# Read orders of the moving operand in the feed-forwards, shifted split weights, and an odd output in 256-token halves

## The reference

```python
def _swiglu(h, w_gate, w_up, w_down):
    return (jax.nn.silu(h @ w_gate) * (h @ w_up)) @ w_down

for layer in range(DEPTH):                       # DEPTH = 2
    h = _rmsnorm(x, ffn1_norm[layer])
    x = x + 0.5 * _swiglu(h, ffn1_w_gate[layer], ffn1_w_up[layer], ffn1_w_down[layer])
    h = _rmsnorm(x, mix_norm[layer])
    ...                                          # even: h @ even_w_in, SSD and S5, @ even_w_out
    ...                                          # odd: h @ odd_w_in, attention and pooling, @ odd_w_out
    x = x + mixed.astype(x.dtype)
    h = _rmsnorm(x, ffn2_norm[layer])
    x = x + 0.5 * _swiglu(h, ffn2_w_gate[layer], ffn2_w_up[layer], ffn2_w_down[layer])
```

## Time and profile before

| | |
|---|---|
| time, median of 2 runs | 2786.28 us (2784.91 and 2787.65) |
| span of the profiled execution | 2784.2 us |
| TensorE busy | 2711.2 us (97%), 12920 products |
| weight loads | 2210.3 us (79%) |
| VectorE busy | 1423.6 us (51%) |
| ScalarE busy | 964.3 us (35%) |
| GpSimd busy | 220.7 us (8%) |
| DMA | 282.71 MB, mean 102 GB/s |

### The profile page before, as it was taken

The page is one execution under the profiler, slowest core; times in us unless marked ns, Lnnn a source line. Parts: engine busy times, 40 slices in busy tenths (PEclk is TensorE's granted clock), DMA queues, the critical chain, the costliest instruction groups (busy, mean ns, idle before and its releaser), DMA issues. The chain is left out here.

```text
span 2784.2 us, 34074 instructions
## 1 busy us (share of the span) xinstructions
PE 2711.2 (97%) x12920; PEld 2210.3 (79%) x12920; DVE 1423.6 (51%) x1824; ACT 964.3 (35%) x1354; POOL 220.7 (8%) x212
## 2 busy tenths in 40 slices
PE   8999999899999999999999999999999999999998
PEld 6878887678888888888766888888888777788887
DVE  6676248655443344443485544432898535633334
ACT  5433223643332233322235333322333642423312
POOL 2000114020000000000221000000000000300003
PEclk9999999999999999999999999999999999999999
DMA  4334425233323222332311223333442023222331
GB/s 152 119 118 141 137 95 174 70 106 106 98 98 106 91 90 92 98 116 88 110 61 46 98 98 95 113 109 109 136 145 76 19 89 129 83 92 97 109 100 56
DMA packets 78079, 282.71 MB, mean 102 GB/s; under 512 B 10256, under 2 KB 10896, under 8 KB 77216
## 3 DMA queue, kind: packets, MB, share of 16 engines
q1 hardware_dynamic: 67520, 249.67, 27.5%
q0 software_dynamic: 5856, 25.47, 2.6%
q10 hardware_dynamic: 4608, 6.30, 0.9%
HBM read 261.21 MB, written 13.89 MB: 99 GB/s over the span
## 5 line engine op out<-in xcount | busy, mean ns | idle before, releaser
L190 DVE TENSOR_TENSOR wl<-raw,wh 128x1024 fp32r<-128x1024 f32 (+2 forms) x439 | 565.7, 1289 | 1048.9 <-ACT wh L184 1048.0
L236 PE MATMUL PS<-Hh,wl 128*128 128x512 f32 x2160 | 846.1, 392 | 20.0 <-DVE wl L190 16.1
L184 ACT ACTIVATE wh<-raw 128x1024 fp32r<-128x1024 f32 (+2 forms) x440 | 480.2, 1092 | 1044.5 <-PE PS L238 885.1
L238 PE MATMUL PS<-Hl,wh 128*128 128x512 f32 x2160 | 840.8, 389 | 0.0
L237 PE MATMUL PS<-Hh,wh 128*128 128x512 f32 x2160 | 840.7, 389 | 0.0
L236 PEld LDWEIGHTS PS<-Hh,wl 128*128 128x128 f32 x2160 | 405.5, 188 | 117.9 <-issue 25.2
L238 PEld LDWEIGHTS PS<-Hl,wh 128*128 128x128 f32 x2160 | 405.5, 188 | 84.9
L237 PEld LDWEIGHTS PS<-Hh,wh 128*128 128x128 f32 x2160 | 405.6, 188 | 83.5 <-issue 1.0
L236 PE MATMUL PS<-ffn_gh,wl 128*128 128x512 f32 x880 | 342.7, 389 | 0.0
L238 PE MATMUL PS<-ffn_gl,wh 128*128 128x512 f32 x880 | 342.3, 389 | 0.0
L237 PE MATMUL PS<-ffn_gh,wh 128*128 128x512 f32 x880 | 342.3, 389 | 0.0
(11 more groups left out here) (487 smaller groups left out, 2571.9 us busy)
## 6 DMA issues: line engine op xcount, KB each, us to landing
raw<-in_gu SPq DMA_DIRECT2D x220, 512.0 KB, 3.4
raw<-in_dn SPq DMA_DIRECT2D x80, 704.0 KB, 4.1
raw<-in_hin SPq DMA_DIRECT2D x44, 512.0 KB, 3.5
raw<-in_oin SPq DMA_DIRECT2D x16, 512.0 KB, 3.5
raw<-in_hin_gate SPq DMA_DIRECT2D x16, 512.0 KB, 3.5
X<-QKV ACTq DMA_DIRECT2D x96, 64.0 KB, 2.0
kept_x<-X POOLq DMA_DIRECT2D x16, 256.0 KB, 3.6
raw<-in_eout SPq DMA_DIRECT2D x8, 512.0 KB, 4.4
```

The lines of the kernel that those rows point to most:

```text
L184: self.nc.scalar.activation(self.wh[j % SPLIT][:, 0:kw], self.raw[j][:, 0:kw], ACT.Copy).then_inc(self.hi_ready, 1)
L190: self.nc.vector.tensor_sub(self.wl[j % SPLIT][:, 0:kw], self.raw[j][:, 0:kw], self.wh[j % SPLIT][:, 0:kw].bitcast(F32)).then_inc(self.lo_ ...
L236: self.nc.tensor.matmul(out, wl, xh[:, u.k0 + k, :], start=first, stop=False)
L238: done = self.nc.tensor.matmul(out, wh, xl[:, u.k0 + k, :], start=False, stop=last)
```

## The change

No product of the feed-forwards is added or taken away, and their order on TensorE stays. What changes is how one product walks through its 512 tokens. TOKENS has three orders: up (0, 1, 2, ...), down (511, 510, ...) and halves (groups of four neighbours, taken by turns from the lower and the upper 256 tokens, each half from its end to its start: 252 to 255, 508 to 511, 248 to 251, ...). The moving operands and the PSUM output use the same order, so each result stays in its place. FFN_ORDERS gives each feed-forward the order of its first stage, a shift of the split weights in that stage (0, 4, 8 or 16 elements of 4 bytes: wh and wl are written and read so much later in their tiles) and the order of its second stage:

| feed-forward | first stage | shift in bytes | second stage |
|---|---|---|---|
| 0 | down | 0 | down |
| 1 | halves | 0 | halves |
| 2 | halves | 16 | up |
| 3 | halves | 32 | up |
| 4 | halves | 64 | up |

In the odd mixer's output each chunk is multiplied in two parts of 256 tokens: the three products for the first 256, then the three for the last 256, each with a weight load of its own. All other stages keep order and shift.

```diff
--- before.py
+++ after.py
@@ -50,12 +50,20 @@
         self.bank, self.start, self.stop = bank, start, stop
 
 
+TOKENS = {
+    "up": (0, [[1, S]]),
+    "down": (S - 1, [[-1, S]]),
+    "halves": (S // 2 - 4, [[-4, S // 8], [S // 2, 2], [1, 4]]),
+}
+
+
 class Stage:
 
 
 
-    def __init__(self, bodies, units, chunks, banks):
+    def __init__(self, bodies, units, chunks, banks, order="up", shift=0):
         self.bodies, self.units, self.chunks, self.banks = bodies, units, chunks, banks
+        self.order, self.shift, self.parts = order, shift, 1
         self.base = None
         self.begun = False
         self.tokens = {}
@@ -176,19 +184,32 @@
         if k + 1 < len(self.stages):
             self.load_turn(sp, self.stages[k + 1], 0)
 
+    def weights(self, t, st, k):
+
+        return t[:, st.shift + k * P:st.shift + (k + 1) * P]
+
+    def tokens_of(self, t, st, p=0):
+
+        if st.parts > 1:
+            n = S // st.parts
+            return t[:, p * n:(p + 1) * n]
+        first, dims = TOKENS[st.order]
+        return bass.AP(t.tensor, t.offset + first, [list(t.ap[0])] + dims)
+
     def split_hi(self, act, st, i, j):
 
         kw = st.units[j].kc * P
         act.wait_ge(self.raw_in[j], 16 * (st.base // RAW + 1) + 16 * i)
         act.wait_ge(self.unit_done, st.base + j + 1 + RAW * i)
-        self.nc.scalar.activation(self.wh[j % SPLIT][:, 0:kw], self.raw[j][:, 0:kw], ACT.Copy).then_inc(self.hi_ready, 1)
+        self.nc.scalar.activation(self.wh[j % SPLIT][:, st.shift:st.shift + kw], self.raw[j][:, 0:kw], ACT.Copy).then_inc(self.hi_ready, 1)
 
     def split_lo(self, dve, st, i, j):
 
         kw = st.units[j].kc * P
         dve.wait_ge(self.hi_ready, st.base + j + 1 + RAW * i)
-        self.nc.vector.tensor_sub(self.wl[j % SPLIT][:, 0:kw], self.raw[j][:, 0:kw],
-                                  self.wh[j % SPLIT][:, 0:kw].bitcast(F32)).then_inc(self.lo_ready, 1)
+        at = slice(st.shift, st.shift + kw)
+        self.nc.vector.tensor_sub(self.wl[j % SPLIT][:, at], self.raw[j][:, 0:kw],
+                                  self.wh[j % SPLIT][:, at].bitcast(F32)).then_inc(self.lo_ready, 1)
 
     def multiply(self, pe, st, bank_free, operand=None, after=0, between=None, chunk_ready=None):
 
@@ -226,16 +247,17 @@
                 if operand:
                     pe.wait_ge(operand[0], operand[1][j])
                 xh, xl = u.x
-                out = self.PS[:, u.bank, :]
                 for k in range(u.kc):
                     if chunk_ready and j == 0:
                         pe.wait_ge(chunk_ready, k + 1)
-                    wh = self.wh[j % SPLIT][:, k * P:(k + 1) * P]
-                    wl = self.wl[j % SPLIT][:, k * P:(k + 1) * P]
+                    wh, wl = (self.weights(t[j % SPLIT], st, k) for t in (self.wh, self.wl))
                     first, last = u.start and k == 0, u.stop and k == u.kc - 1
-                    self.nc.tensor.matmul(out, wl, xh[:, u.k0 + k, :], start=first, stop=False)
-                    self.nc.tensor.matmul(out, wh, xh[:, u.k0 + k, :], start=False, stop=False)
-                    done = self.nc.tensor.matmul(out, wh, xl[:, u.k0 + k, :], start=False, stop=last)
+                    for p in range(st.parts):
+                        out, hi, lo = (self.tokens_of(t, st, p) for t in (
+                            self.PS[:, u.bank, :], xh[:, u.k0 + k, :], xl[:, u.k0 + k, :]))
+                        self.nc.tensor.matmul(out, wl, hi, start=first and p == 0, stop=False)
+                        self.nc.tensor.matmul(out, wh, hi, start=False, stop=False)
+                        done = self.nc.tensor.matmul(out, wh, lo, start=False, stop=last and p == st.parts - 1)
                 done.then_inc(self.unit_done, 1)
                 if between:
                     between(RAW * i + j)
@@ -283,17 +305,18 @@
             pe.wait_ge(self.lo_ready, nxt.base + j + 1)
             bank_read(pe, u.bank)
         xh, xl = u.x
-        out = self.PS[:, u.bank, :]
         for n, k in enumerate(chunks):
             if chunk_ready:
                 pe.wait_ge(chunk_ready, k + 1)
-            wh = self.wh[j % SPLIT][:, k * P:(k + 1) * P]
-            wl = self.wl[j % SPLIT][:, k * P:(k + 1) * P]
+            wh, wl = (self.weights(t[j % SPLIT], nxt, k) for t in (self.wh, self.wl))
             start = first and u.start and n == 0
             stop = last and u.stop and n == len(chunks) - 1
-            self.nc.tensor.matmul(out, wl, xh[:, u.k0 + k, :], start=start, stop=False)
-            self.nc.tensor.matmul(out, wh, xh[:, u.k0 + k, :], start=False, stop=False)
-            done = self.nc.tensor.matmul(out, wh, xl[:, u.k0 + k, :], start=False, stop=stop)
+            for p in range(nxt.parts):
+                out, hi, lo = (self.tokens_of(t, nxt, p) for t in (
+                    self.PS[:, u.bank, :], xh[:, u.k0 + k, :], xl[:, u.k0 + k, :]))
+                self.nc.tensor.matmul(out, wl, hi, start=start and p == 0, stop=False)
+                self.nc.tensor.matmul(out, wh, hi, start=False, stop=False)
+                done = self.nc.tensor.matmul(out, wh, lo, start=False, stop=stop and p == nxt.parts - 1)
         if last:
             done.then_inc(self.unit_done, 1)
 
@@ -424,16 +447,20 @@
             co.run(dve, st, co.split_lo, read, (lambda: scale.dve(dve)) if scale else None)
 
 
+FFN_ORDERS = [("down", 0, "down"), ("halves", 0, "halves"), ("halves", 4, "up"), ("halves", 8, "up"), ("halves", 16, "up")]
+
+
 def plan_ffn(co, k):
+    up_order, shift, down_order = FFN_ORDERS[k]
     gu, dn = co.dram[f"gu{k}"], co.dram[f"dn{k}"]
     x = (co.Hh, co.Hl)
     up = co.plan(Stage(FC // 2, [
         Unit(DC, lambda i, j=j: gu[bass.ds(RAW * i + j, 1)].rearrange("o p n -> p (o n)"), x, 0, j) for j in range(RAW)
-    ], 2, 2))
+    ], 2, 2, up_order, shift))
     down = co.plan(Stage(DC // 2, [
         Unit(HALF, lambda i, j=j: dn[bass.ds(RAW * i + j, 1)].rearrange("o p n -> p (o n)"), None, HALF * (j % 2),
              4 + j // 2, j % 2 == 0, j % 2 == 1) for j in range(RAW)
-    ], 2, 2))
+    ], 2, 2, down_order))
     return up, down
 
 
@@ -1001,8 +1028,9 @@
             res.pool(pool)
             pool.wait_ge(co.lo_ready, nxt.base + 1)
             pool.wait_ge(co.hi_ready, nxt.base + 2)
-            nc.gpsimd.tensor_sub(co.wl[1][:, 0:DC * P], co.raw[1][:, 0:DC * P],
-                                 co.wh[1][:, 0:DC * P].bitcast(F32)).then_inc(co.lo_ready, 1)
+            at = slice(nxt.shift, nxt.shift + DC * P)
+            nc.gpsimd.tensor_sub(co.wl[1][:, at], co.raw[1][:, 0:DC * P],
+                                 co.wh[1][:, at].bitcast(F32)).then_inc(co.lo_ready, 1)
             res.part_by_pool(pool)
 
         @block.scalar
@@ -2693,7 +2721,9 @@
 def plan_odd(co):
     st = feed(co, "oin")
     st.tokens = {3: (lambda t: slice(t * P, (t + 1) * P), 0, 0)}
-    return st, feed(co, "oout")
+    out = feed(co, "oout")
+    out.parts = 2
+    return st, out
 
 
 def odd_mixer(co, plan, cols, gain):
```

## The result

| | before | after |
|---|---|---|
| time, median of 2 runs | 2786.28 us | 2925.16 us (2923.49 and 2926.84) |
| span of the profiled execution | 2784.2 us | 2924.7 us |
| ratio | | 1.050, 95% interval 1.0483 to 1.0517 |

The changed kernel is 138.9 us slower; the forecast was 2807 us, 20.7 us slower, and its range ended at 2860. Here are stretches of the changed kernel: start and end, length, busy us (and instructions) of TensorE, weight loads, VectorE, ScalarE and GpSimd, then granted clock and DMA.

What follows compares the result with a forecast made beforehand. TensorE was taken as the bound, products times start distance. Span 2784.2 + 18.1 (feed-forward orders) + 2.6 (odd output) = 2804.9 us, plus 2.1 from span to median, gave 2807.0 us; range 2745 to 2860.

Steps and rivals of the forecast that it cites:

- What bounds the kernel: Whole kernel: TensorE is the limit; time is the number of products times the distance between their starts, usually 226.7 ns.
- That the usual value is the lowest: Product distance on TensorE: 226.7 ns, a 13.3 ns surplus over 213.4, is the lowest of any steady stretch.
- The size of part 1: Feed-forward orders and shifts: +2.85 ns on each of 6336 products, +18.1 us, within bounds of -84 and +53 us.
- D: Rival, feed-forward 0: backward reads or writes are slow in themselves; half rate on 1584 products, +317 us, 3106 us; chance 0.17.
- The term of the odd output: Odd mixer's output: 192 products become 384 of 256 columns, the surplus is paid twice per pair, +2.6 us.
- The lower bound by bare loads: Odd output: weight loads 111 ns apart make a pair at least 222 ns, -0.9 us.
- the other signs: Signs of being right: 227 to 235 ns in changed stretches, 226.7 in untouched down products, odd output near 120, TensorE 100 busy.
- The sign of being wrong in kind: TensorE idle before products released by a split, or weight loads longer than 188 ns in a changed stage.
- Cost nothing for the splits: VectorE and ScalarE splits in shifted stages: hidden behind a unit of 24 products (5.44 us), so no cost.
- A: The forecast itself: changed feed-forward orders fall somewhat worse, 2807 us, alone 2790 to 2842; chance 0.40.
- C: Rival: changed orders make weight and token reads meet less; half the surplus gone 2746.8 us, all 2704.5; chance 0.15.
- The Trainium skill's two rules: SBUF: a new 16-byte line every access is punished, two hits are not; PSUM: non-contiguous patterns slow products significantly.

## Why the prediction was wrong

**What bounds the kernel** held: TensorE is busy without a gap in the windows of the changed stages, and the time is products times distance, but for feed-forward 0's first stage, whose pauses took up 4 us. The counts held too (6336 products walked anew).

**That the usual value is the lowest** held for every order of the change, so the direction was right, but not as a rule: leaps of 4 groups of 8 had 220.0 ns in the first three units of their stage.

**The size of part 1** is the step that failed. The forecast took the middle between 226.7 and 232.4, +2.85 ns on each of 6336 products, and called 235.1 the upper bound of a changed order. Measured: +6.6 for 1584 backward products and +26.6 to +29.6 for 4752 in halves, +135.2 us in the table where the sum has +18.1. The reason that was given, that whole runs of four neighbours, or one neighbour after another, can fall into the usual step, is what the runs refute: four neighbours and a leap cost 26.6 ns, and of all orders that turn back or leap only those in runs of 64 tokens (256 bytes) or more kept 226.7 through a stage. The rows behind the bound were of other things: the earlier trace rows is an upward walk with the tokens out of step with the weights, an upward walk beside strided weights. Neither broke the token stream. None of the rows read has 512 tokens out of order (the kernel before has a few short products that leap, of 128 columns in runs of 16 or 32, in lines 1832 and 2614, which weren't priced), and for what the rows don't hold the bound has to come from the nearest row on the expensive side, which here was the half rate priced under D.

**The term of the odd output**: +2.6 us by the working, +2.4 in the trace, 1.0011 in time. The lower bound by bare loads wasn't reached (a pair of loads at 222 ns is 4.7 ns under 226.7, not the 4.5 of the working; the bound stays at -0.9 us). Of the other signs, 226.7 in the untouched second stages and TensorE at 100 were seen too; 227 to 235 ns was seen in feed-forward 0 alone. The sign of being wrong in kind, a load over 188 ns, showed faintly: loads have 191 and 193 ns in the stages shifted by 16 and 32 bytes, and the second of these is no slower for it than the stage without a shift (253.3 both).

**Cost nothing for the splits** held: VectorE's share fell (51 to 49%), and TensorE's wait for a split didn't grow; the page's idle time before these products is 16.2 us, where the earlier trace rows had 20.0:

```profile
L258 PE MATMUL PS<-Hh,wl 128*128 128x512 f32 x2160 | 890.0, 412 | 16.2 <-DVE wl L211 12.4
```

**The reason behind A and C**, reads of weights and tokens meeting, was mostly wrong. Backward and halved orders keep all or most of their price with a quarter of the weights loaded or a single column repeated. It was right in one place, the upward walk, where being in step with the weights is worth 6.6 ns (226.7 against 233.3) and weights four apart cost 8.3 (235.0, as in the earlier trace rows).

**D** was the rival on the right side of the range, for the wrong place, mechanism and price. It expected backward steps to be dear, with feed-forward 0 stretched and the rest not, and decided from +35 ns on; that feed-forward had +6.6 ns and cost +6.5 us in all. The dear part was the interleaving in the four others, for which I had argued that neighbours by fours are enough. It's the same belief that made D unlikely (a step to the neighbour is harmless): nearly true for backwards, false for a leap after four tokens.

**The Trainium skill's two rules** that stood in the prediction don't hold here. The Trainium skill's page PSUM — Partial Sum Buffer (Specifications) has any non-contiguous pattern slow down products; here products written backwards or in fours from two halves stay at 226.7 ns. The Trainium skill's page SBUF — State Buffer (Specifications) asks for two hits on each 16-byte line; reading every second token has two hits a line and takes 453.3 ns, twice the usual, and four hits in a line didn't save halves from 253.3. The measurements decide.

**Still open**: why loops over 16 and 32 tokens, or swapped groups of 8, cost more than longer walks; why leaps of 8, 16 and 32 groups differ; why the upward walk alone pays by product and looks at where the weights lie; and what a pause of TensorE can change, so that the same order over the same tiles stands 226.7 or 233.3, 246.7 or 253.3, 220.0 or 230.7 ns apart before and behind it. So the distance of one stretch needn't be the order's only one, and differences of 6.7 ns between two orders are less certain than those of 20 and more. A product without any weight load wasn't tried, as these products bring their load with them.

## What to carry to other kernels

Read the distance between starts of products, per stage, not their recorded length or TensorE's busy share: 5 per cent hid behind a share of 100.00 in both kernels. Let the moving operand run upwards through whole runs of 256 bytes; beyond that the order was free, on the PSUM side it was free in every form tried, and steps of two elements cost twice the time. Put moving tiles and weights at the same place within 256 bytes (worth 5 to 7 ns on an upward walk here). And where a change does what no row shows, take the bound from the dear side, however far its row seems.

## What the runs showed of the hardware

- A product of 512 tokens at full clock: 216.7 ns with one token, or the same 4 or 8, repeated; 226.7 walking upwards in step with the weights; 229 to 234 upwards out of step; 233.3 backwards; 246.7 to 253.3 by turns from two halves in groups of 4, 250 to 254 in groups of 8; 331 in groups of 2; 453 with step 2. Groups of 8 in leaps have anything from 220.0 to 258.9.
- The same order over the same tiles can have two steady distances; they changed at pauses of TensorE (226.7 and 233.3 with weights shifted by 16 bytes, 246.7 and 253.3 in halves, 220.0 and 230.7 in leaps of 4 groups of 8).
- Runs of 256 bytes, each read upwards from 128 bytes past a multiple of 256, keep 226.7 ns in any order tried: backwards, interleaved, in leaps.
- The columns loaded as weights, 32, 64 or 128, changed the recorded load (108 ns for 32, 138 for 64, 188 for 128) and left the distance backwards at 233.3.
- The lower clock has no surplus: 427 ns for 512 columns.
- PSUM may be written in another order than the tokens are read, backwards or interleaved, at no cost in distance.
